# Zero columns of weight pieces, taps beside pooling and the order of norms in a two-block transformer kernel

## The reference

```
for l in 0, 1:
    shift, scale, gate (6 each) = silu(cond) @ w_mod[l] + b_mod[l]
    h, hc = modulate(rms_norm(x)), modulate(rms_norm(xc))
    q, k, v, u_pool, a, b = split(h @ w_in[l])       # and the same of hc
    attn = differential attention over keys and values of both streams
    conv = silu(layer_norm(depthwise_conv31(a * sigmoid(b))))
    pool = (windowed means of u_pool, minus u_pool) @ pool_w
    x  = x + g1 * (concat(attn, pool, conv) @ w_out[l])
    x  = x + g2 * (silu(g) * u) @ w_ffn_out[l],  g, u = split(modulate(rms_norm(x)) @ w_ffn_in[l])
    # xc likewise, in layer 0 only
```

## Time and profile before

| | |
|---|---|
| median of 3 runs | 1782.28 us (1781.27 to 1784.9) |
| the profiled execution | 1783.53 us |
| its span | 1781.6 us |
| mean granted clock | 0.974 |
| busy: TensorE, VectorE, ScalarE, GpSimd | 1670.4, 1066.5, 890.6, 193.2 us |
| moved by DMA | 301.04 MB |

### The profile page before, as it was taken

The page is one execution under the profiler, slowest core; times in us unless marked ns, Lnnn a source line. Parts: engine busy times, 40 slices in busy tenths (PEclk is TensorE's granted clock), DMA queues, the critical chain, the costliest instruction groups (busy, mean ns, idle before and its releaser), DMA issues. The chain is left out here.

```text
span 1781.6 us, 30262 instructions
## 1 busy us (share of the span) xinstructions
PE 1670.4 (94%) x12864; PEld 1508.0 (85%) x12864; DVE 1066.5 (60%) x1472; ACT 890.6 (50%) x1192; POOL 193.2 (11%) x138
## 2 busy tenths in 40 slices
PE   5889988999999999998899999988999999889999
PEld 2777656999999999865899989767999997679999
DVE  2498566644455445976644445756776456557773
ACT  2334555644345434555544345654655356555652
POOL 1140000122003210300022100000101000000110
PEclk7999989999999999998999999999999999999999
DMA  9233645466546555473266554302555533025553
GB/s 370 96 143 139 241 169 213 189 238 242 187 167 215 191 175 184 144 265 115 100 226 203 175 175 146 120 25 96 191 182 193 190 119 128 24 93 193 189 188 123
DMA packets 45110, 301.04 MB, mean 169 GB/s; under 512 B 5216, under 2 KB 7360, under 8 KB 11696
## 3 DMA queue, kind: packets, MB, share of 16 engines
q1 hardware_dynamic: 44304, 297.57, 47.1%
q0 software_dynamic: 240, 0.79, 0.1%
q10 hardware_dynamic: 432, 0.75, 0.1%
HBM read 298.02 MB, written 1.06 MB: 168 GB/s over the span
## 5 line engine op out<-in xcount | busy, mean ns | idle before, releaser
L1757 DVE TENSOR_TENSOR wl<-raw,wh 128x2064 fp32r<-128x2064 f32 (+3 forms) x236 | 532.7, 2259 | 508.1 <-ACT wh L1531 458.0
L1531 ACT ACTIVATE wh<-raw 128x2064 fp32r<-128x2064 f32 (+3 forms) x236 | 440.3, 1869 | 247.6 <-PE bank L1343 149.1
L1338 PE MATMUL bank<-hx_hi,wh 128*128 128x256 f32 x1920 | 546.2, 285 | 16.3 <-ACT hx_hi L1531 9.7
L1341 PE MATMUL bank<-hx_hi,wl 128*128 128x256 f32 x1920 | 537.9, 280 | 4.4 <-DVE wl L1757 4.4
L1343 PE MATMUL bank<-hx_lo,wh 128*128 128x256 f32 x1920 | 538.1, 280 | 0.0
L1338 PEld LDWEIGHTS bank<-hx_hi,wh 128*128 128x128 f32 x1920 | 365.2, 190 | 24.2 <-issue 20.0
L1341 PEld LDWEIGHTS bank<-hx_hi,wl 128*128 128x128 f32 x1920 | 365.0, 190 | 10.2 <-DVE wl L1757 5.7
L1343 PEld LDWEIGHTS bank<-hx_lo,wh 128*128 128x128 f32 x1920 | 364.6, 190 | 0.7 <-DVE hx_lo L1749 0.4
L1341 PE MATMUL bank<-hid_hi,wl 128*128 128x256 f32 x880 | 244.9, 278 | 1.7 <-DVE wl L1757 1.5
L1338 PE MATMUL bank<-hid_hi,wh 128*128 128x256 f32 x880 | 244.6, 278 | 0.0
L1343 PE MATMUL bank<-hid_lo,wh 128*128 128x256 f32 x880 | 244.3, 278 | 0.0
(11 more groups left out here) (208 smaller groups left out, 1962.4 us busy)
## 6 DMA issues: line engine op xcount, KB each, us to landing
raw<-in_wts SPq DMA_DIRECT2D x208, 1032.0 KB, 4.8
raw<-in_wts SPq DMA_DIRECT2D x50, 1024.0 KB, 6.2
raw<-in_wts SPq DMA_DIRECT2D x20, 776.0 KB, 4.3
raw<-in_wts SPq DMA_DIRECT2D x4, 584.0 KB, 3.9
tmp<-tscr SPq DMA_DIRECT2D x16, 128.0 KB, 4.4
raw<-in_wts SPq DMA_DIRECT2D x2, 648.0 KB, 4.5
xTc<-in_ctxT SPq DMA_DIRECT2D x1, 1024.0 KB, 10.8
xTx<-in_xT SPq DMA_DIRECT2D x1, 1024.0 KB, 8.6
```

Source lines behind the costliest of these rows:

```text
L1338: pe.matmul(out, block(hi, k, ncols, c, m), x_hi, start=first and k == 0 and o == 0, stop=False, skip_group_check=True)
L1341: pe.matmul(out, block(lo, k, ncols, c, m), x_hi, start=False, stop=False, skip_group_check=True)
L1531: return act.activation(out, in_, func, bias=bias, scale=scale)
L1757: tt(M.wl[k][:, 0:ne], M.raw[f["r"]][:, 0:ne], M.wh[k][:, 0:ne].bitcast(F32), ALU.subtract).then_inc(*on.inc(f["tlo"]))
```

## The change

The zero columns stay behind the first block only in some pieces: all of in1, in2, uq and out, the first two up pieces of each stage, some further up pieces of the first block and the first dn piece of each stage. In all others they stand in front of all blocks (step 0), so that every block begins 64 bytes past a multiple of 128 bytes. mod and ukv have none, as before (None). The size of a piece stays.

```
+    def up(j, first):
+        return 2048, 256 if j < 2 or first else 0
+    def down(kb, first):
+        return (2048, 2048, 1536)[kb], 256 if first else 0
-        keys += [(("up1", l, j), 2048, 256) for j in range(22)]
-        keys += [(("dn1", l, ch, kb), (2048, 2048, 1536)[kb], 256) for ch in range(4) for kb in range(3)]
+        keys += [(("up1", l, j), *up(j, j % 2 == 0 if l else j % 4 == 2)) for j in range(22)]
+        keys += [(("dn1", l, ch, kb), *down(kb, ch == kb == 0)) for ch in range(4) for kb in range(3)]
...
+        keys += [(("up2", l, j), *up(j, False)) for j in range(22)]
+        keys += [(("dn2", l, ch, kb), *down(kb, ch == kb == 0)) for ch in range(4) for kb in range(3)]
...
-    def block(w, k, ncols, c, m):
-        at = k * ncols + (STEP if k else 0) + c
+    def block(f, w, k, ncols, c, m):
+        at = k * ncols + (STEP if k or not f["step"] else 0) + c
```

The first mod group looks ahead only in its first four pieces, part p and the c stream of q0 get 4 taps and every other turn 10, and both norms of the start come together:

```
-        f = take(("mod", l, cb, k), look=k < 7)
+        f = take(("mod", l, cb, k), look=k < (4 if (l, cb) == (0, 0) else 7))
...
+                pooling = part == "p" or part == "q0" and s == streams[0]
                 pump(2)
                 run_pending()
-                pump(7)
+                pump(2 if pooling else 8)
...
-    toks["c"] = finish0("c")
     p.look()
     for pr in range(4):
         n["x"].add(pr, t_x["x"])
-    def start_x():
-        n["x"].root()
-        toks["x"] = finish0("x")
-        lambdas()
-    before_x.append(start_x)
+    for s in "cx":
+        toks[s] = finish0(s)
+    before_x.append(lambdas)
```

```
-    two.pop(0)()
+    for three in [fn() for fn in two]:
+        three()
+    step("log_set")
     pc_split("c", "c")
-    weave(chain(steps(lambda: two.pop(0)()), attention1(0, "x", "x")),
-          chain(steps(idle), outproj1(0, "c", "c", BY_COLS, norm)),
+    weave(attention1(0, "x", "x"),
+          outproj1(0, "c", "c", BY_COLS, norm),
...
         scores(0)
+        exps(0)
         yield
-        exps(0)
```

A new step "log_set" loads the Ln/Exp table on ScalarE if it isn't in place:

```
+    def log_set():
+        if table[0] != LOG_SET:
+            act.preload_act_table_set(LOG_SET)
+        table[0] = LOG_SET
```

More of the change, by code:

```diff
@@ L292, in dma @@
             r = n % NRAW
-            row, ne, _ = self.PT[self.pieces[n]]
+            row, ne, step = self.PT[self.pieces[n]]
             t = self.ev(f"raw{r}", 16)
             self.step("piece", r=r, row=row, ne=ne, free=self.raw_free[r], t=t)
-            self.info[n] = {"r": r, "ne": ne, "tok": t}
+            self.info[n] = {"r": r, "ne": ne, "step": step, "tok": t}
             self.n_dma += 1
@@ L642, in two, with three @@
             tmps.give(rs, t_n)
-            conv_tok[s] = [t_x[1]]
+            def three():
+                t_x = [ev("cact"), ev("cact")]
+                step("conv3", l=l, s=s, t_n=t_n, t_x=t_x)
+                conv_tok[s] = [t_x[1]]
+            return three
         return two
@@ L799, in ffn_down @@
         return nrm, t
+    behind = []
     def ffn1(l, s, toks, fill=None):
@@ L811, in ffn1 @@
             step("silu", b=bg_, tk=tg, sl=sl, free=sl.free, t=a)
+            if i == 10 or i == 0 and behind:
+                step("log_set")
             banks.give(bg_, a)
@@ L924, in plan_program @@
     weave(ox)
-    behind = [lambda: finish_ffn_in("x")]
+    behind.append(lambda: finish_ffn_in("x"))
     def ffn_step(i):
@@ L953, in plan_program, with norm_half @@
     keys, proj, piece = (lambda: next(gc)), (lambda: next(gx)), (lambda: next(out))
-    norm_half, mix_half = (lambda: two.pop(0)()), (lambda: pc_split("x", "c"))
+    def norm_half():
+        two.pop(0)()()
+        step("log_set")
+    mix_half = lambda: pc_split("x", "c")
     fill = ((keys, proj), (proj, keys), (proj, conv_half), (norm_half, mix_half), (piece,), (piece,))
@@ L1337, in gemm @@
                     on.wait_ge(free[j])
-                pe.matmul(out, block(hi, k, ncols, c, m), x_hi, start=first and k == 0 and o == 0, stop=False,
+                pe.matmul(out, block(f, M.wh, k, ncols, c, m), x_hi, start=first and k == 0 and o == 0, stop=False,
                           skip_group_check=True)
                 on.wait_ge(f["tlo"])
-                pe.matmul(out, block(lo, k, ncols, c, m), x_hi, start=False, stop=False, skip_group_check=True)
+                pe.matmul(out, block(f, M.wl, k, ncols, c, m), x_hi, start=False, stop=False, skip_group_check=True)
                 on.wait_ge(a_toks[k0 + k][1])
-                ins = pe.matmul(out, block(hi, k, ncols, c, m), x_lo, start=False, stop=last and k == nk - 1,
+                ins = pe.matmul(out, block(f, M.wh, k, ncols, c, m), x_lo, start=False, stop=last and k == nk - 1,
                                 skip_group_check=True)
@@ L1353, in gemm_tok @@
                 on.wait_ge(a_toks[k][0])
-                pe.matmul(out, a[0][:, k, sl], block(hi, k, 256, 0, 256), start=k == 0 and j == 0, stop=False, skip_group_check=True)
+                pe.matmul(out, a[0][:, k, sl], block(f, M.wh, k, 256, 0, 256), start=k == 0 and j == 0, stop=False, skip_group_check=True)
                 on.wait_ge(f["tlo"])
-                pe.matmul(out, a[0][:, k, sl], block(lo, k, 256, 0, 256), start=False, stop=False, skip_group_check=True)
+                pe.matmul(out, a[0][:, k, sl], block(f, M.wl, k, 256, 0, 256), start=False, stop=False, skip_group_check=True)
                 on.wait_ge(a_toks[k][1])
-                ins = pe.matmul(out, a[1][:, k, sl], block(hi, k, 256, 0, 256), start=False, stop=k == nk - 1, skip_group_check=True)
+                ins = pe.matmul(out, a[1][:, k, sl], block(f, M.wh, k, 256, 0, 256), start=False, stop=k == nk - 1, skip_group_check=True)
         ins.then_inc(*on.inc(t))
@@ L2138, in put @@
     def put(key, a):
-        row, n, first = PT[key]
-        if first:
-            out[row, :, 0:first], out[row, :, first + STEP:n] = a[:, 0:first], a[:, first:]
+        row, n, step = PT[key]
+        if step is None:
+            out[row, :, 0:n] = a
         else:
-            out[row, :, 0:n] = a
+            out[row, :, 0:step], out[row, :, step + STEP:n] = a[:, 0:step], a[:, step:]
     def common(l, w_out, up, dn, n):
```

35 lines of the change are left out of this document (18 added, 17 removed).

## The result

The changed kernel takes 1770.93 us in the median of 4 runs (1766.72 to 1772.92), the kernel before, on the same chip, 1781.93: a ratio of 0.9934 with a 95% interval of 0.9914 to 0.9954. That is 11 us less, where 27 were forecast. The profiled execution has a span of 1770.4 us.

A forecast was written before the change was run, and what follows sets the result against it. The prediction took TensorE, busy 94% of the span, as the bound, with gains from its pitch, waits and low-clock stretches. Its terms summed to 27.2 us off the profiled 1783.5, giving a median of 1756 us, range 1742 to 1771.

The forecast's parts named there:

- Part 1: 135 feed-forward pieces with zero columns in front of all blocks: no slow first matmuls, 10.0 us gained (3.8 to 14).
- nothing new is late: Densest stretch: a faster TensorE needs weights 0.075 us sooner per piece; VectorE busy 80.9 of 104.9 us, DMA 55%.
- part 5: Norms and stage ends: table loads of 1.28 us run ahead of need; gains 2.0, 1.3, 1.0, 1.3, losses 1.3 twice.
- Part 2: Kernel start: x's root before c's first gemm, which hides x's normalisation; 2.0 us gained (-1 to 3.5).
- Part 3: Beside pooling: 4 taps a turn instead of 9 end the k0 wait, 6.0 us (3 to 6.7); layer 1, 1.2.
- Part 4: Convolution norms together, early first exponentials, attention at once: out's c gemm starts earlier, near 222.5; 5.0 us gained (1 to 10).
- The first two stages: First two feed-forward stages: table load runs while ScalarE is idle; 2.0 us (1.3 to 3) and 1.3 gained.
- layer 1's gemm: Layer 1's first gemm for x: third place of the late-load pattern, with a wait of 1.1 us; 1.0 gained.
- the seam: Norm at the seam to the second block, on the path with TensorE idle: early table load gains 1.3 us.
- the load behind the silus: Layer 1: load stands ahead of the split whose gemm TensorE idles for until 802.31; 1.3 us lost (0 to -1.3).
- The load behind the last gate: Second block, ahead of down-stage splits: 1.3 us paid, offset by the norm between layers (0); last stage loses 1.3.
- C: Rival: order around pooling and attention costs what it saves; parts 2 to 4 bring 4, not 14.2; 1766 us, chance 0.13.

The follow-up runs named there:

- the later gate: Changed kernel with the previous turn's gate, in the second block's up stages, put behind the second gemm and its split: 1758.45 us, ratio 0.9853.

## Why the prediction was wrong

The direction was right, and 1770.93 lies at the very end of the range, but the change brought 11 of 27 us. By its own steps, in us of lead in the profiled executions:

- **Part 1, the columns: 10.0 forecast, 7.1 measured alone** in the profile (9.1 by the runs, 5.5 to 12.7). The pitch was right to the hundredth (5.44 us). The step that failed is the sentence that nothing new is late, since VectorE is busy 80.9 of 104.9 us. A busy share of 77% bounds what an engine could do, not when it gets its inputs: a loop through VectorE and ScalarE of 11.34 us a pair set the pace, and the later gate showed it by removing it. That took 3 us of this part, and it made part 5's load dear.
- **Part 2, the start: 2.0 forecast, 1.0 measured at the start of the second gemm and 2.8 at its end and at 98.7.** Right. c's gemm started at 50.78 and x's ended at 62.09.
- **Part 3, taps: 6.0 forecast, 7.0 in the profile, and 6 by undoing it.** Right. In layer 1, 0.8 for 1.2. The 2.6 us of fall 2 had no term in the sum.
- **Part 4: +5.0 forecast, -3.9 measured between 178.6 and 296.** This is the largest miss. The wait of 6.80 us for the exponentials is gone as forecast, but out's c gemm started at 229.8 and not at 222.5. The step that failed is what comes before out's first piece: I did not see that with one mod piece fewer there the look-ahead puts the piece's split ahead of the last copies of c's attention, in a stretch where the DMA engines are 99% busy. Undoing that alone gave back only 3.0 of the 7.3 us missing by 288.7, since the wait for the exponentials then came back. The other 1.6, up to 296, went where a split waits for its transfer again; no run undoes that. Also, early exponentials act in layer 1 as well, and there I had given them no price at all: 4.8 us, shown by undoing them there alone.
- **Part 5, table loads: +5.6 - 1.3 - 1.3 forecast.** The first two stages gained 2.6 and 1.2, layer 1's gemm 1.1, the seam 1.2: 6.1 for 5.6, and between 770 and 802, with layer 1's exponentials put back, 1.3 is lost, as I had given the load behind the silus there. The load behind the last gate was the right suspicion with too small a price: in a loop with no slack it cost 3 us a stage instead of 1.3.

Of the rivals, C (the order gives back what it saves) comes nearest, at its time of 1766, but its reason fits in part only: falls 2 and 3 stand behind VectorE's taps, while fall 1 hangs on transfers, and fall 4 on a loop in which VectorE idles. What stays open: what else holds k and modT at 168, where one tap less shortens each wait by 0.4 us; how much of what is missing between 178 and 289 the regrouped norms cost by themselves, since I didn't run them alone; and the 3.8 us lost between 284 and 296, which is read from a timeline and not shown by undoing it.

## What to carry to other kernels

Before you give a faster engine its gain, follow one round of the pipeline from an instruction to the same instruction a turn later, through every in-order queue; if its period is longer than the engine's own, the gain ends when the lead is used up, however idle the others look. Waits that begin only towards the end of a stage can be the sign of such a loop. A step moved earlier in an in-order list takes its own waits along, so ask of each place that it acts in (both layers here) what stands behind it.

## What the runs showed of the hardware

The pitch of TensorE's 128 x 128 by 256 matmuls depends on where the stationary block lies: 113.3 ns in a piece whose blocks all begin 64 bytes past a multiple of 128, 119 in one whose blocks all begin at one, and in a mixed piece the slow pitch goes on for some ten matmuls behind the last slow block. The Trainium skill, "SBUF — State Buffer", section "SBUF: two separate sides", says that TensorE waits on no other engine there. The prediction said that the trace disagrees with this; the two can both hold, for the difference is one of place within one buffer, and no run here shows what in the memory makes it.
